# A fused decoder block on one core: the opening expert pair without its gather, and all pairs behind three branches

## The reference

```python
h = rms_norm(x); proj = h @ w_in                  # retention and mLSTM, two parallel mixers
x = x + (sigmoid(gate_r) * y_ret + sigmoid(gate_m) * y_m) @ w_out
h2 = rms_norm(x)
g_w, g_idx = top_k(softmax(h2 @ w_group + b_group), 1)          # one of 4 groups
top_logits, e_idx = top_k(the group's 8 expert logits, 2)       # two of its 8 experts
weights = g_w * softmax(top_logits)
out = sum over the 2 experts of weights * (silu(h2 @ w_gate[e]) * (h2 @ w_up[e])) @ w_down[e]
return rms_norm(x + out) * norm_final_w
```

## Time and profile before

| | us |
|---|---|
| median of 3 runs | 1087.26 (1085.89 to 1087.49) |
| the profiled execution | 1088.14 |
| its span, first to last instruction | 1086.4 |
| TensorE busy | 1013.1 (93%) |
| DVE, ACT, GpSimd busy | 425.0, 276.6, 70.4 |
| moved by DMA | 263.83 MB |

### The profile page before, as it was taken

How to read it: one execution, slowest core, us unless ns; L and a number is a source line. 1 busy time by engine, 2 the same in 40 slices (tenths; PEclk the granted TensorE clock), 3 DMA queues, 4 the chain that set the end, 5 groups by cost and what they waited for, 6 DMA issues and landing times.

```text
span 1086.4 us, 12967 instructions
## 1 busy us (share of the span) xinstructions
PE 1013.1 (93%) x4661; PEld 649.7 (60%) x4661; DVE 425.0 (39%) x733; ACT 276.6 (25%) x462; POOL 70.4 (6%) x102
## 2 busy tenths in 40 slices
PE   4999999999999999999993999999999999889874
PEld 4888888888888888888883333333333333333322
DVE  4236356434533334535524123333333232333316
ACT  5343564433333336413221000000000000000002
POOL 0564000000000000000000000000000000000000
PEclk9999999999999999999995999999999999999978
DMA  7313222222222222245829799999999999999791
GB/s 273 116 55 141 78 78 78 78 78 78 78 78 78 93 101 79 77 127 171 328 109 395 303 421 420 420 421 421 421 421 420 420 417 421 421 420 418 303 383 78
DMA packets 59959, 263.83 MB, mean 243 GB/s; under 512 B 9152, under 2 KB 9216, under 8 KB 35208
## 3 DMA queue, kind: packets, MB, share of 16 engines
q1 hardware_dynamic: 57432, 257.94, 60.2%
q0 software_dynamic: 2480, 5.26, 1.3%
HBM read 263.17 MB, written 4.20 MB: 246 GB/s over the span
## 4 chain that ended last, share of the span: by engine, by line
PE 55%; DMA 39%; issue 2%; DVE 2%; SPq 1%; ACT 0%; DVEq 0%; POOLq 0%; ACTq 0%
PE pj L463 45%; DMA raw_moe<-in_w_gate_dram 13%; DMA raw_moe<-in_w_up_dram 13%; DMA raw_moe<-in_w_down_dram 12%; PE pj L650 2%; PE cb L429 2%; DMA xg<-x_scratch,tok_tab 1%; PE cb L608 1%; PE cb L482 1%; PE pj L676 1%; PE cb L508 1%; DMA vrow<-in_mlstm_conv_w_dram 1%; PE cb L550 1%; PE cb L512 0%; PE cb L515 0%
## 5 line engine op out<-in xcount | busy, mean ns | idle before, releaser
L650 PE MATMUL pj<-raw_moe,xT 128*64 128x512 f32 x1024 | 233.0, 604 | 25.2 <-issue 10.2
L1070 DVE TENSOR_TENSOR wl<-raw_mix,wh 128x1024 fp32r<-128x1024 f32 x88 | 109.1, 1245 | 183.3 <-ACT wh L807 183.0
L650 PEld LDWEIGHTS pj<-raw_moe,xT 128*64 128x64 f32 x1024 | 75.1, 139 | 168.0 <-issue 168.0
L463 PE MATMUL pj<-wh,hTh 128*128 128x512 f32 x320 | 130.1, 407 | 1.6 <-DVE hTl L1098 1.6
L463 PE MATMUL pj<-wl,hTh 128*128 128x512 f32 x320 | 125.3, 392 | 0.0
L463 PE MATMUL pj<-wh,hTl 128*128 128x512 f32 x320 | 125.0, 391 | 0.0
L807 ACT ACTIVATE wh<-raw_mix 128x1024 fp32r<-128x1024 f32 x88 | 92.4, 1057 | 121.9 <-PE pj L463 111.1
L1403 DVE TENSOR_TENSOR x<-x,cb 128x512 f32<-128x512 f32 x120 | 77.0, 683 | 103.7 <-PE cb L687 103.7
L676 PE MATMUL pj<-raw_moe,hf 128*64 128x512 f32 x512 | 116.7, 598 | 0.8 <-ACT hf L1018 0.8
L463 PE MATMUL pj<-hTh,wh 128*128 128x512 f32 x192 | 80.2, 418 | 0.0
L463 PE MATMUL pj<-hTh,wl 128*128 128x512 f32 x192 | 75.4, 393 | 0.0
(11 more groups left out here) (274 smaller groups left out, 1217.4 us busy)
## 6 DMA issues: line engine op xcount, KB each, us to landing
raw_moe<-in_w_gate_dram SPq DMA_DIRECT2D x64, 1024.0 KB, 9.7
raw_moe<-in_w_up_dram SPq DMA_DIRECT2D x64, 1024.0 KB, 10.1
raw_moe<-in_w_down_dram SPq DMA_DIRECT2D x64, 1024.0 KB, 9.7
raw_mix<-in_w_in_dram SPq DMA_DIRECT2D x32, 1024.0 KB, 5.0
raw_mix<-in_w_ret_branch_dram SPq DMA_DIRECT2D x4, 1024.0 KB, 5.1
raw_mix<-in_w_mlstm_branch_dram SPq DMA_DIRECT2D x4, 1024.0 KB, 5.6
raw_mix<-in_w_out_dram SPq DMA_DIRECT2D x4, 1024.0 KB, 5.2
xt<-in_x_dram SPq DMA_DIRECT2D x4, 512.0 KB, 5.2
```

Of the source, the lines that this page charges most:

```text
L463: m = nc.tensor.matmul(pj[:, i, :], lhsT, rhs, start=k == 0 and n == 0, stop=k == KD - 1 and n == 2)
L650: mm = nc.tensor.matmul(pj[a * CAP:(a + 1) * CAP, up, :], xT[:, 4 * half + k, a * CAP:(a + 1) * CAP], raw_moe[(m + a) % MOE_RAW][:, k, :], ...
L1070: V.tensor_tensor(wl[:, q % RING, :, :], raw_mix[n % MIX_RAW][:, 2 * (q % 2):2 * (q % 2) + 2, :], wh[:, q % RING, :, :].bitcast(F32), ALU. ...
```

## The change

1. **Branches.** All sixteen pairs of a round now stand behind the branches of further rounds. The loop of seven passes becomes three conditions in a row, for round 1, for rounds 2 and 3, and for rounds 4 to 7. Each of them holds its own code of a round (all pairs of round r-1, then tables and first gate product of round r). Ahead of them stand, on TensorE, only the token table and the opening pair's gate product; behind them `all_pairs(extra)`, that is slot table, the opening pair's up and down products and all other pairs, with `extra` from a register. SP, whose last 12 chunks join the others of the round, has its branches behind all 192 chunks.
2. **The opening pair.** Its rows are no longer gathered. DVE makes `pair_hot`, the one-hot of the tokens against the 128 slots of experts 0 and 1, from `ppos` (which moves from `cb` bank 1 to `pj` bank 3); TensorE multiplies the stream tiles in SBUF with it, 2 x 4 x 4 products of 128x128x128 in float32, straight into the two banks that `turn_x` would fill.
3. **Order on DVE.** The longest list is read out earlier (`cnt_ok`), the copies to `xT` stand around `weights()`, and the number of further rounds follows with its own semaphore (`rounds_ok`).
4. **Weights.** The 18 buffers are laid out anew; chunks 8 to 11 are issued ahead of the store of the stream, 12 to 17 behind it, and no chunk waits for the logits. For that `h2T` and `squares` move, and two squares wait for the one before.
5. **A sigmoid that loads its table** moves on ACT from behind the exponents to behind the branches.

```diff
+        def further_rounds(eng, most, one_round):
+            for lo, hi in ((1, 2), (2, 4), (4, ROUNDS)):
+                with eng.If(most > lo * CAP):
+                    if hi - lo == 1:
+                        one_round(lo)
+                    else:
+                        with eng.Fori(lo, hi, 1) as r:
+                            one_round(r)
...
@@ sync
-            for m in range(8, 16):
+            sp.wait_ge(wl_ok, MIX_PAIRS)
+            moe_chunk(8, 0, 0, False)
+            moe_chunk(9, 0, 0, False)
+            wait_mix_pair(sp, MIX_PAIRS - 3)
+            moe_chunk(10, 0, 0, False)
+            moe_chunk(11, 0, 0, False)
...
+            for m in range(12, MOE_RAW):
                 moe_chunk(m, 0, 0, False)
-            sp.wait_ge(lg_ps, 1)
-            for m in range(16, MOE_RAW):
-                moe_chunk(m, 0, 0, False)
             round_chunks(0)
             sp.wait_ge(cnt_ok, 1)
             most = sp.value_load(cnt[0:1, 0:1], min_val=0, max_val=T)
-            with sp.Fori(1, ROUNDS, 1) as r:
-                with sp.If(most > r * CAP):
-                    round_chunks(r)
-            extra = sp.value_load(cnt[0:1, 1:2], min_val=0, max_val=ROUNDS - 1)
-            for m in range(LAST_CHUNKS, R_CHUNKS):
-                moe_chunk(m, extra, 0, True)
+            further_rounds(sp, most, round_chunks)
@@ tensor
+            pe.wait_ge(ph_ok, 1)
+            for part in range(2):
+                for k in range(4):
+                    for t in range(TT):
+                        m = nc.tensor.matmul(cb[:, part, k * P:(k + 1) * P], x2[:, t, 512 * part + k:512 * (part + 1):4], pair_hot[:, t, :],
+                                             start=t == 0, stop=t == TT - 1)
+                m.then_inc(xT_ps, 1)
...
+            def all_pairs(r):
+                N0 = r * PAIRS
+                slot_table(r)
                 for half in range(2):
-                    gate_or_up(r, 0, 0, 1, half)
+                    gate_or_up(r, 0, 0, 1, half, first=True)
...
+            def one_round(r):
+                all_pairs(r - 1)
+                combine(r * PAIRS - 1, range(8))
+                token_table(r)
+                turn_x(r * PAIRS, 0)
+                turn_x(r * PAIRS, 1)
+                first_gate(r)
+
+            token_table(0)
+            first_gate(0)
             pe.wait_ge(cnt_ok, 1)
             most = pe.value_load(cnt[0:1, 0:1], min_val=0, max_val=T)
-            with pe.Fori(1, ROUNDS, 1) as r:
-                with pe.If(most > r * CAP):
-                    moe_round(r)
-
+            further_rounds(pe, most, one_round)
+            pe.wait_ge(rounds_ok, 1)
             extra = pe.value_load(cnt[0:1, 1:2], min_val=0, max_val=ROUNDS - 1)
-            last_pair(extra)
+            all_pairs(extra)
@@ vector
+            away = rt[:, 7, 56:56 + 2 * TT].rearrange("p (t a) -> p t a", a=2)
+            dve.wait_ge(hot_in, 1)
+            own(V.tensor_scalar(away, hot16[:, :].rearrange("p (t e) -> p t e", e=NE)[:, :, 0:2], -float(NO_TOKEN), float(NO_TOKEN), ALU.mult, ALU.add))
             dve.wait_ge(pos_ps, 1)
...
+            own(V.tensor_tensor(away, away, ppos[:, :, 0:2], ALU.add))
+            V.tensor_tensor(pair_hot[:, :, :].rearrange("p t (a s) -> p t a s", a=2), away.unsqueeze(3).to_broadcast([P, TT, 2, CAP]),
+                            iot[:, :].unsqueeze(1).unsqueeze(1).to_broadcast([P, TT, 2, CAP]), ALU.is_equal).then_inc(ph_ok, 1)
...
+                if is_first(r):
+                    x_copy(0, 0)
+                    weights()
+                    x_copy(0, 1)
                 dve.wait_ge(tab_ps, r * 2 + 2)
@@ gpsimd
-            def moe_round(r):
+            def all_pairs(r):
                 N0 = r * PAIRS
...
-                pool.wait_ge(tab_ok, r + 1)
-                gather(N0, 0)
                 gather(N0 + 1, 1)
```

More of the change, by code:

```diff
@@ L384, in round_chunks @@
                         moe_chunk(m, r, i, True)
-                for m in range(MOE_RAW + SP_LOOPS * 2 * MOE_RAW, LAST_CHUNKS):
+                for m in range(MOE_RAW + SP_LOOPS * 2 * MOE_RAW, R_CHUNKS):
                     moe_chunk(m, r, 0, True)
@@ L636, in turn_x, with gate_or_up @@
                 m.then_inc(xT_ps, 1)
-            def gate_or_up(r, i, n, up, half):
+            def gate_or_up(r, i, n, up, half, first=False):
                 N, m = r * PAIRS + i * LOOP_PAIRS + n, PAIR_CHUNKS * n + 4 * up + 2 * half
@@ L642, in gate_or_up @@
                     pe.wait_ge(xT_ok, N * 2 + (half + 1))
-                if half == 0 and (not isinstance(N, int) or N > 0):
+                if half == 0 and not first:
                     pe.wait_ge((q_ok, h_ok)[up], N)
@@ L661, in turn_h, with down @@
                 m.then_inc(ht_ps, 1)
-            def down(r, i, n, half):
+            def down(r, i, n, half, first=False):
                 N, m = r * PAIRS + i * LOOP_PAIRS + n, PAIR_CHUNKS * n + 8 + 2 * half
@@ L986, in square @@
                 act.wait_ge(free[t], BLOCKS)
[L987 removed]
+                if t >= 2:
+                    act.wait_ge(sq_ok, 3 * TT + t - 1)
+                nc.scalar.activation(squares[t % 2][:, :], x2[:, t, :], ACT.Square, accum_out=ssq[:, t:t + 1]).then_inc(sq_ok, 1)
             def stream_copy(t):
@@ L1409, in x_copy, with pair @@
                                 ALU.mult).then_inc(xT_ok, 1)
-            def pair(N, first=False, last=False, bare=False):
+            def pair(N, last=False, bare=False):
                 dve.wait_ge(now_ok, N + 1)
@@ L1434, in pair, with tables @@
                                            ALU.mult, ALU.subtract).then_inc(yl_ok, 1)
-            def moe_round(r):
+            def tables(r):
                 N0 = r * PAIRS
-                if not isinstance(r, int):
-                    pair(N0 - 1, last=True)
-                    add(N0 - 1, range(8))
+                if not is_first(r):
                     dve.wait_ge(it_ok, r)
@@ L1462, in moe_round @@
                 dve.wait_ge(wt_ps, r * 2 + 2)
                 V.tensor_copy(slot_tab[:, :, 1:3].rearrange("p n c -> p c n"), cb[:, 3, 0:NE].rearrange("p (c n) -> p c n", c=2)).then_inc(wt_ok, 1)
-                x_copy(N0, 0)
-                x_copy(N0, 1)
-                pair(N0, first=isinstance(r, int), bare=True)
+                pair(N0, bare=True)
                 with dve.Fori(0, PAIRS - 2, 1) as i:
                     pair(N0 + i + 1)
-            moe_round(0)
+                pair(N0 + (PAIRS - 1), last=True)
@@ L1472, in _, with one_round @@
+            def one_round(r):
+                all_pairs(r - 1)
+                add(r * PAIRS - 1, range(8))
+                tables(r)
+            tables(0)
+            dve.wait_ge(ir_in, 16)
             most = dve.value_load(cnt[0:1, 0:1], min_val=0, max_val=T)
-            with dve.Fori(1, ROUNDS, 1) as r:
-                with dve.If(most > r * CAP):
-                    moe_round(r)
+            further_rounds(dve, most, one_round)
+            dve.wait_ge(rounds_ok, 1)
             extra = dve.value_load(cnt[0:1, 1:2], min_val=0, max_val=ROUNDS - 1)
-            pair(extra * PAIRS + (PAIRS - 1), last=True)
+            all_pairs(extra)
@@ L1581, in moe_round, with one_round @@
                     columns(N0 + i + 1, i + 1)
-            moe_round(0)
+                columns(N0 + (PAIRS - 1), PAIRS - 1)
+            pool.wait_ge(tab_ok, 1)
             pool.wait_ge(cnt_ok, 1)
             most = pool.value_load(cnt[0:1, 0:1], min_val=0, max_val=T)
-            with pool.Fori(1, ROUNDS, 1) as r:
-                with pool.If(most > r * CAP):
-                    moe_round(r)
+            def one_round(r):
+                all_pairs(r - 1)
+                pool.wait_ge(tab_ok, r + 1)
+                gather(r * PAIRS, 0)
+            further_rounds(pool, most, one_round)
+            pool.wait_ge(rounds_ok, 1)
             extra = pool.value_load(cnt[0:1, 1:2], min_val=0, max_val=ROUNDS - 1)
-            columns(extra * PAIRS + (PAIRS - 1), PAIRS - 1)
+            all_pairs(extra)
 def constants():
@@ L1615, in constants @@
     k[:, K_PRIO:K_PRIO + NE] = NE - np.arange(NE)
-    k[:, K_LIMIT:K_LIMIT + ROUNDS - 1] = CAP * np.arange(1, ROUNDS)
+    for r in range(1, ROUNDS):
+        k[:, K_LIMIT + r - 1] = CAP * 2 ** (r.bit_length() - 1)
     k[:, K_ROW:K_ROW + T] = np.arange(T)
```

99 lines of the change are left out of this document (45 added, 54 removed).

## The result

The changed kernel takes 1093.58 us (median of 18 runs, 1089.6 to 1095.16) against 1087.54 us of the kernel before on the same chips: ratio 1.0055, 95% interval 1.0047 to 1.0063, that is **6.0 us slower**. Forecast were 1084.5 us, in a range of 1074 to 1091.

The account below looks back on a forecast made before the run. In the expert phase the weight stream (about 421 GB/s) was taken as the bound, so idle DMA time is lost time. End -10.9 plus opening +8.1 gave -2.8 us: 1085.3 profiled, 1084.5 median, range 1074 to 1091.

Parts of the forecast that it names:

- The end: Last pair: without SP's branches the chunks run on and the last down product ends 10.9 us earlier (9.5 to 13.1).
- The opening, one-hot products: Opening pair: one-hot products replace the gather, so chunks 0 and 1 are used at 598.8 instead of 603.9 us.
- Rival 2: Opening: one-hot products at half clock throughout, gate half ending at 606.4; total +3.7 us, 1091.0 us; chance 0.10.
- The opening, three branches: Between opening gate and up product: TensorE's three skips each pay a code fetch, 14.3 us in all (7.2 to 19.8).
- rival 3: Between opening gate and up product: every skip pays the full 6.6 us, 19.8 in all; total +2.7, 1090.0 us; chance 0.20.
- The half clock behind the pause: Opening up half, after TensorE's idling at the branches: 4.2 us at half clock from 615.9, up half ending at 622.0.
- The sum: Opening loses 8.1 us (chunk 22 flows at 623.4, before 615.3), end gains 10.9: total -2.8 us.
- What was costed at nothing: Chunks' new order, two waiting squares, sigmoid's table load, pair 1's later gather, and waits on a register: each 0 us.

Follow-up runs that it names:

- neighbouring columns: Changed kernel with one-hot products taking 128 neighbouring columns as stationary tile instead of every fourth column: 1087.44 us, ratio 1.0000 against the kernel before.
- the nested: Changed kernel with its three branches nested, so one skip instead of three: 1077.68 us, ratio 0.9918 against the kernel before.
- the short bodies: Changed kernel with three conditions in a row whose bodies only increment a semaphore: 1079.21 us, ratio 0.9927 against the kernel before.
- the gather so quickened: Changed kernel with nested branches and the opening pair's rows gathered instead of one-hot products, new chunk order kept: 1073.4 us, ratio 0.9882 against the kernel before.
- copied tiles: Changed kernel with nested branches, one-hot products reading a stream that ACT copied into side-by-side columns: 1072.96 us, ratio 0.9873 against the kernel before.

## Why the prediction was wrong

**The end: right.** -10.9 us were forecast. SP's issue of chunk 179 ends at 1029.20 us (1021.41 + 7.79) where it ended at 1013.37, 15.8 us later, and the last down product ends 4.8 us later: between the two the changed kernel is 11.0 us shorter. The waits against a register in all pairs cost nothing that shows. One slip in its bounds changes nothing: the lower one took 2.9 us for the cold clock, where the 10.9 us two paragraphs earlier leave 13.39 - 10.9 = 2.5.

**The opening, one-hot products: the step that failed.** I took "64 instructions ... 0.11 us each" at full clock from a product whose stationary tile lay in one piece. The stationary tile here takes every fourth column, its load takes 329 ns, and the instructions come 0.235 us apart at either clock: 15.20 us instead of 9.4. With neighbouring columns the same 64 took 9.93, so count and operation were right, the clock nearly, and the layout of the operand was left out. It moved the first use of chunks 0 and 1 from the forecast 598.8 to 605.1, later than the 603.9 of the gather, and the gain of the step became a loss. Rival 2 had this size, 15.6 us, but by the wrong mechanism: the clock was full again from 591. With the products near the forecast (neighbouring columns) the kernel takes 1087.4 us, so this step holds some 6 of the 9.1 us by which the forecast was off.

**The opening, three branches: right in kind, too small.** That each skip pays, and that the stream then stands behind chunk 21, was forecast and is shown by the nested and the short bodies. The sum was 14.3 us, measured 16.6: the first smaller (3.4 for 6.6, the engines being idle when it began), the second and third larger (8.1 and 5.1 for 5.3 and 2.4). That is 2.3 us in the direction of rival 3, whose turning point of 17.1 us the sum did not reach: alone, this would have left the forecast at 0.5 us faster than the kernel before.

**The half clock behind the pause: too small.** I took 4.2 us of it from the opening, where TensorE resumes at 597.07. It was 6 us, and the first up half, forecast to end 6.1 us after the products resume, took 7.6. The nearer row was the pause at the end of the same trace, with 5.8 us at half clock behind it:

```profile
1044.20:1045.20 1.00, 1.00 (x5) 0.55 1.00 410
```

**The sum.** Forecast: chunk 22 flows at 623.4. Measured 631.2 (it is issued at 630.2, and the share of 0.41 from 630 to 632 makes 0.8 us of flow), 7.8 us later. The whole gate product ends at 608.2 and not at 602.4, 5.8 us from the products. The fetches add 2.3 and the longer half clock 1.5. Taken off are 0.8, since the sequencer ran 4.4 us ahead of the engine and not 3.6, and 1.0 in small steps (the further conditions, the second read, issue and start). -2.8 + 7.8 is +5.0, and the profiled executions differ by 4.8.

**What was costed at nothing.** No run has the change with the old order of the chunks, so that it is worth nothing there is not shown. With the gather in place it is worth 4.3 us. Against the gather so quickened the opening pair's products win nothing that can be told: 0.4 us less from copied tiles (1072.96 and 1073.4), 4.3 more with every fourth column.

The Trainium skill's rule in "Runtime: NRT & Kernel Launch", section "Instruction fetch mechanics", that a taken branch out of the window stalls for a fetch, agrees with three skips of 3.4, 8.1 and 5.1 us over long bodies and of 0.22 to 0.34 us over short ones.

## What to carry to other kernels

Put rarely taken code behind one condition and nest the others in it: skips in a row over long bodies each paid here (13.7 to 17.4 us for three), and all but 1.2 us of a single one of 3.8 us was hidden, since the sequencer met it before the engine had finished. Beside the full stream a single one took 6.3 us and left 4.85 of idling. Before a path is replaced because a transfer on it is slow, ask what else is in the transfer's way: moving the reads out of the way of the gather gained as much as the replacement could. When a duration is borrowed from another product, compare the strides of the stationary tile too, and take the half clock behind a pause from a pause of like length.

## What the hardware showed that I had not expected

- The load of a 128x128 float32 stationary tile with every fourth column took 329 ns against 192 for neighbouring columns, in float32 products, and these came 0.235 us apart whatever the clock. The turns with such a tile did not show it (16 in 1.93 us, at full clock), so no row of the kernel before gave a warning.
- A skip right behind a skip is dearer, 5.0 us against 3.6 with hardly used DMA engines, and 7.6 to 8.1 beside the weights.
- A strided copy of 128x512 on ACT took 1.10 us; the copies of that size that read neighbouring columns, from PSUM where this one reads SBUF, took 0.60.
